# The first projection of an encoder block by blocks of 128 tokens, with the norm weight as a column scale of the weights' two parts

## What is computed

```python
h = rmsnorm(x, g_mix)                       # x / rms(x) * g_mix, per token
proj = h @ w_in                             # 512 x 1024 by 1024 x 3584
qa, ka, va, qb, kb, vb, gate_a, gate_b = split(proj)
oa = global_axial_gqa(...); ob = window_sink_gqa(...)
merged = sigmoid(gate_a) * (oa @ w_branch_a) + sigmoid(gate_b) * (ob @ w_branch_b)
x = x + merged @ w_out
x = x + moe(rmsnorm(x, g_ffn), ...)         # top 4 of 32 experts
out = rmsnorm(x, g_final)
```

## Time and profile before

| what | value |
|---|---|
| median of 3 runs | 1559.31 us (1558.9 to 1561.21) |
| the profiled execution | 1559.76 us, of which the span of the trace is 1558.0 us |
| mean granted PE clock | 0.986 |
| first matmul of the projection | 18.18 us |
| PE idle between its transposes and that matmul | 4.32 us |
| group 0 of the projection ends, group 1 begins | 42.50 us |

### The profile page before, as it was taken

How to read it: one execution, slowest core, us unless ns; L and a number is a source line. 1 busy time by engine, 2 the same in 40 slices (tenths; PEclk the granted TensorE clock), 3 DMA queues, 4 the chain that set the end, 5 groups by cost and what they waited for, 6 DMA issues and landing times.

```text
span 1558.0 us, 21230 instructions
## 1 busy us (share of the span) xinstructions
PE 1512.6 (97%) x7254; PEld 1240.9 (80%) x7287; DVE 1311.9 (84%) x1021; ACT 1091.1 (70%) x1158; POOL 268.3 (17%) x164
## 2 busy tenths in 40 slices
PE   7999999997999999999999999999999999999997
PEld 6888788886788888888888888888888888888884
DVE  4556587656899999999999999999999999999975
ACT  4344587424787777877777787787777778778772
POOL 6302144100001110111100001202120022002211
PEclk9999999998899999999999999999999999999997
DMA  8330001545999999999999999999999999999972
GB/s 299 122 100 36 1 1 55 200 141 181 378 363 391 385 389 385 379 391 379 375 387 386 386 387 381 388 390 385 376 372 391 386 378 394 387 387 380 388 263 113
DMA packets 131102, 477.36 MB, mean 306 GB/s; under 512 B 9720, under 2 KB 10240, under 8 KB 130976
## 3 DMA queue, kind: packets, MB, share of 16 engines
q1 hardware_dynamic: 117536, 434.79, 72.1%
q0 software_dynamic: 9936, 36.44, 9.1%
q10 hardware_dynamic: 3600, 5.73, 1.1%
HBM read 452.81 MB, written 24.12 MB: 306 GB/s over the span
## 4 chain that ended last, share of the span: by engine, by line
PE 93%; DVE 3%; ACT 2%; issue 1%; DMA 0%; ACTq 0%; SPq 0%; DVEq 0%
PE ps L1446 28%; PE ps L1447 28%; PE ps L1448 28%; PE ps L1708 2%; PE ps L1716 2%; PE ps L1735 2%; PE ps L1494 1%; PE ps L1537 1%; DVE pT_lo L1155 1%; PE ps L1538 0%; ACT probs L754 0%; PE ps L1479 0%; DMA xs<-in_x 0%; DVE split L1068 0%; PE ps L1515 0%
## 5 line engine op out<-in xcount | busy, mean ns | idle before, releaser
L1279 DVE TENSOR_TENSOR chunk_lo<-chunk,chunk_hi 128x2048 fp32r<-128x2048 f32 x384 | 859.3, 2285 | 39.0 <-ACT chunk_hi L879 36.0
L879 ACT ACTIVATE chunk_hi<-chunk 128x2048 fp32r<-128x2048 f32 x378 | 722.6, 1914 | 109.2 <-PE ps L1448 108.1
L1446 PE MATMUL ps<-chunk_hi,XT 128*128 128x512 f32 x1024 | 404.8, 395 | 2.0 <-DVE XT L1324 2.0
L1448 PE MATMUL ps<-chunk_hi,XT 128*128 128x512 f32 x1024 | 400.0, 391 | 0.0
L1447 PE MATMUL ps<-chunk_lo,XT 128*128 128x512 f32 x1024 | 399.9, 391 | 0.0
L644 POOL DMA_INDIRECT sum_rows<-y,idx x31 | 116.4, 3755 | 921.7 <-ACT y L985 833.8
L1446 PEld LDWEIGHTS ps<-chunk_hi,XT 128*128 128x128 f32 x1024 | 192.8, 188 | 41.1 <-DVE XT L1324 2.4
L1448 PEld LDWEIGHTS ps<-chunk_hi,XT 128*128 128x128 f32 x1024 | 192.4, 188 | 40.4
L1447 PEld LDWEIGHTS ps<-chunk_lo,XT 128*128 128x128 f32 x1024 | 192.8, 188 | 38.9
L1446 PE MATMUL ps<-chunk_hi,hidT 128*128 128x512 f32 x512 | 200.4, 391 | 0.0
L1448 PE MATMUL ps<-chunk_hi,hidT 128*128 128x512 f32 x512 | 200.1, 391 | 0.0
(11 more groups left out here) (272 smaller groups left out, 1900.7 us busy)
## 6 DMA issues: line engine op xcount, KB each, us to landing
chunk<-in_w_gate_up SPq DMA_DIRECT2D x256, 1024.0 KB, 8.8
chunk<-in_w_down SPq DMA_DIRECT2D x128, 1024.0 KB, 7.1
raw<-in_w_in SPq DMA_DIRECT2D x14, 1024.0 KB, 6.8
xs<-in_x SPq DMA_DIRECT2D x8, 512.0 KB, 5.2
w_out<-in_w_out SPq DMA_DIRECT2D x4, 1024.0 KB, 6.8
raw<-in_w_branch_a SPq DMA_DIRECT2D x2, 1024.0 KB, 6.0
raw<-in_w_branch_b SPq DMA_DIRECT2D x2, 1024.0 KB, 6.9
sum_rows<-xs ACTq DMA_DIRECT2D x4, 512.0 KB, 2.6
```

Of the source, the lines that this page charges most:

```text
L879: a.activation(chunk_hi[hi_slot(c, nxt)][:, :], chunk[c][:, :], ACT.Copy).then_inc(ex_hi, 1)
L1279: v.tensor_tensor(chunk_lo[c][:, :], chunk[c][:, :], chunk_hi[hi_slot(c, nxt, first)][:, :].bitcast(F32), ALU.subtract).then_inc(ex_lo, 1)
L1446: mm(dst, lhsT(0), rhs(0), start=start, stop=False)
L1448: return mm(dst, lhsT(1), rhs(0), start=False, stop=stop)
```

## The change

The chunks of the weights are now scaled: `gcol` goes into both parts of the weights (per k block of 512 columns, so each split is four instructions of 128x512 instead of one of 128x2048) and out of the transposed tokens. The tokens are normalised, transposed (two PSUM banks each, 4 and 5 or 6 and 7) and split one block at a time; PE starts block 0 of the projection with token block 0 alone and transposes the next token block in the middle of each of the blocks n = 0, 1, 2. Chunks 0 and 1 are split in halves with a count of `in_lo` for each half (`split_parts` turns a number of chunks into that count). SP loads x block 0, chunk 0, x block 1, chunk 1, x blocks 2 and 3, chunks 2 and 3. The five small DMAs of ACT's queue stand behind the split of chunk 2. Core of the diff:

```diff
@@ SP
-            for c in range(NT):
-                sp.dma_start(xs[:, c, :], x_v[c]).then_inc(x_in[c], 16)
+            load_x(0)
+            load_chunk(0)
+            load_x(1)
+            load_chunk(1)
+            load_x(2)
+            load_x(3)
+            load_chunk(2)
+            load_chunk(3)
+            for n in range(NIN, CHUNKS - 2):
+                sp.wait_ge(in_lo, split_parts(n - NIN + 1))
                 load_chunk(n)
@@ ACT
+            def top_part(n, kk):
+                cols = slice(kk * 512, kk * 512 + 512)
+                k = n % 2 * 4 + kk
+                return a.activation(split[:, n % NIN_SPLIT, 0, cols], raw[:, n % NIN, cols], ACT.Copy,
+                                    scale=gcol[:, k:k + 1])
...
-                a.activation(split[:, n % NIN_SPLIT, 0, :], raw[:, n % NIN, :], ACT.Copy).then_inc(in_hi, 1)
+                for kk in range(4):
+                    last = top_part(n, kk)
+                last.then_inc(in_hi, 1)
+            def hT_round(c):
+                act.wait_ge(hT_ps, c + 1)
+                a.activation(hT[:, 0, :, c * 128:(c + 1) * 128],
+                             ps[:, 4 + c % 2 * 2:6 + c % 2 * 2, :].rearrange("p t (k n) -> p (t k) n", n=128),
+                             ACT.Copy).then_inc(hT_hi, 1)
+            mix_root(0)
+            first_in_hi(0, 0)
+            first_in_hi(0, 1)
+            hT_round(0)
+            mix_root(1)
+            first_in_hi(1, 0)
+            first_in_hi(1, 1)
+            hT_round(1)
+            mix_root(2)
+            hT_round(2)
+            mix_root(3)
+            hT_round(3)
+            in_split_hi(2)
+            act.dma_start(rp, rope.rearrange("(c p) t n -> p c t n", p=128)).then_inc(consts_in, 16)
...
@@ DVE
+            def rest_part(n, kk):
+                cols = slice(kk * 512, kk * 512 + 512)
+                k = n % 2 * 4 + kk
+                return v.scalar_tensor_tensor(out=split[:, n % NIN_SPLIT, 1, cols], in0=raw[:, n % NIN, cols],
+                                              scalar=gcol[:, k:k + 1],
+                                              in1=split[:, n % NIN_SPLIT, 0, cols].bitcast(F32), op0=ALU.mult,
+                                              op1=ALU.subtract)
+            def in_split_lo(n):
+                if n >= IN_CHUNKS:
+                    return
+                dve.wait_ge(in_hi, split_parts(n + 1))
+                for kk in range(4):
+                    last = rest_part(n, kk)
+                last.then_inc(in_lo, 1)
+            mix_norm(0)
+            first_in_lo(0, 0)
+            hT_rest(0)
+            first_in_lo(0, 1)
+            mix_norm(1)
+            first_in_lo(1, 0)
+            first_in_lo(1, 1)
+            hT_rest(1)
+            mix_norm(2)
+            hT_rest(2)
+            mix_norm(3)
+            hT_rest(3)
+            in_split_lo(2)
@@ PE
                     for k in range(KD):
-                        if n == 0:
-                            pe.wait_ge(hT_lo, k + 1)
-                        elif n < 4 and k == 0:
-                            pe.wait_ge(hT_lo, KD)
+                        if n < 3 and k == 4:
+                            mix_turn(n + 1)
+                        if n < 4 and k == 0:
+                            pe.wait_ge(hT_lo, n + 1)
                         m = 2 * grp + k // 4
-                        if c == 0 and k % 4 == 0:
-                            pe.wait_ge(in_lo, m + 1)
+                        if n == 0 and k % 2 == 0:
+                            pe.wait_ge(in_lo, k // 2 + 1)
+                        elif c == 0 and k % 4 == 0:
+                            pe.wait_ge(in_lo, split_parts(m + 1))
```

More of the change, by code:

```diff
@@ L323, in encoder_block, with split_parts @@
         chunk_src += [kp(w[0, :, h * 512:(h + 1) * 512]) for h in range(2) for w in (w_branch_a, w_branch_b)]
+        def split_parts(n):
+            return n + min(n, 2)
         def blocks(t, width):
@@ L670, in _, with mix_root @@
             a.activation(warm[:, :], eps[:, :], ACT.Sqrt)
-            for c in range(NT):
+            def mix_root(c):
                 act.wait_ge(x_in[c], 16)
@@ L693, in in_split_hi @@
                     act.wait_ge(proj_ps, 4 * (m // 2) + 4)
-                a.activation(split[:, n % NIN_SPLIT, 0, :], raw[:, n % NIN, :], ACT.Copy).then_inc(in_hi, 1)
[L696 to L703, removed]
+                for kk in range(4):
+                    last = top_part(n, kk)
+                last.then_inc(in_hi, 1)
+            def hT_round(c):
[17 more added lines that the diff above has]
+            act.dma_start(rp, rope.rearrange("(c p) t n -> p c t n", p=128)).then_inc(consts_in, 16)
+            act.dma_start(gains[:, 0, :], qa_norm[0:1, :].to_broadcast([128, HD])).then_inc(consts_in, 16)
+            act.dma_start(gains[:, 1, :], ka_norm[0:1, :].to_broadcast([128, HD])).then_inc(consts_in, 16)
+            act.dma_start(sink[:, :], sink_b[0:1, :].to_broadcast([128, 8])).then_inc(consts_in, 16)
+            act.dma_start(brt[:, :], b_router[0:1, :].to_broadcast([128, E])).then_inc(consts_in, 16)
             def project_out(n):
@@ L1051, in link, with first_in_lo, mix_norm @@
                 dve.wait_ge(dve_step, steps[0])
-            for c in range(NT):
+            def rest_part(n, kk):
[12 more added lines that the diff above has]
+                last.then_inc(in_lo, 1)
+            def first_in_lo(n, half):
+                dve.wait_ge(in_hi, 2 * n + half + 1)
+                for kk in (2 * half, 2 * half + 1):
+                    last = rest_part(n, kk)
+                last.then_inc(in_lo, 1)
+            def mix_norm(c):
                 dve.wait_ge(rt_done, c + 1)
@@ L1057, in _, with hT_rest @@
                 v.tensor_scalar(xn[:, c, :], xs[:, c, :], rstd[:, c:c + 1], None, ALU.mult).then_inc(xn_ready, 1)
[L1058 to L1078, removed]
+            def hT_rest(c):
+                dve.wait_ge(hT_hi, c + 1)
+                cols = slice(c * 128, c * 128 + 128)
+                v.tensor_tensor(hT[:, 1, :, cols],
+                                ps[:, 4 + c % 2 * 2:6 + c % 2 * 2, :].rearrange("p t (k n) -> p (t k) n", n=128),
+                                hT[:, 0, :, cols].bitcast(F32), ALU.subtract).then_inc(hT_lo, 1)
+            dve.wait_ge(gcol_ps, 1)
+            v.tensor_copy(gcol[:, :], ps[:, 7, 0:KD]).then_inc(gcol_ready, 1)
+            mix_norm(0)
[11 more added lines that the diff above has]
+            in_split_lo(2)
             for n in range(NIN_SPLIT, 7):
```

30 lines of the change are left out of this document (15 added, 15 removed).

## The result

The changed kernel takes 1569.62 us (median of 4 runs, 1569.5 to 1569.74); the kernel before, in the same comparison, 1560.07 (4 runs, 1558.9 to 1561.21). The ratio is 1.0048 with a 95% interval of 1.0033 to 1.0064: slower by 0.3 to 0.6%.

The account below looks back on a forecast made before the run. PE's work plus the places where PE stands still bound the kernel; +8.5 at group 1's k = 4, +0.6 cold clock and +0.6 odd chunks gave +9.7 us, 1569.0 on the median, range 1562.5 to 1573.

Parts of the forecast that it names:

- the term of chunk 3: Group 1: DVE's parts of chunks 2 and 3 fall into POOL's chain, so k = 4 starts at 54.15, not 45.60: +8.5 us.
- the clock behind it: Behind k = 4 of group 1: PE, cold from waiting, still runs at half clock; 0 to 1.3 us lost, 0.6 taken.
- the odd chunks: Groups 2 to 6: longer ACT and DVE splits use 0.92 of 0.94 us spare; 0.6 us in all, bounds 0 and 1.3.
- The win of 2 to 3.5 us at the end of group 0: Start: PE begins with token block 0 alone, first matmul near 12.6; group 0 ends at 39 to 40.5, 2 to 3.5 us won.
- The alternation: Chunks 2 and 3: DVE and POOL exclude each other, each gap between DVE's parts admitting one POOL instruction; main case, 0.76, at 1569.
- the case held likelier: Chunk 2's first DVE part comes in the cast behind POOL's first subtraction, so its fourth part ends at 49.4, not 45.2.
- POOL's chain may start up to 1 us earlier, taken as 0: POOL's bias chain, start 25.73: ACT's small DMAs are out of its way; -1 to 0 us, taken as 0.
- the rival of the earlier chain: POOL's chain starts several us earlier, from 20 us, as its loads land sooner; chunk 3 ends near 48.5, total 1564; chance 0.06.
- four or five DVE parts of 0.66: POOL's bias chain: DVE parts of 0.66 us between its instructions delay it; the eighth part, end of chunk 3, comes at 54.1.
- some 0.7 longer: Sign in the profile: POOL's subtractions last some 0.7 us longer than 4.10 beside DVE's parts.
- The doubled form: Rival: DVE's new two-SBUF-operand form needs 2 ns an element, each part 0.5 us longer; total 1583; chance 0.02.
- The rest of the trace the old one, 9 to 10 us later: Sign in the profile: apart from the named places, the trace stays as before, shifted 9 to 10 us later.

Follow-up runs that it names:

- e4: Changed kernel with one wait added on POOL, holding the rest of its bias chain until chunks 2 to 4 are split; 1560.51 us, ratio 0.9993 to before.
- e1: Changed kernel without POOL's eight bias instructions, a memset in their place; 1560.38 us, ratio 0.9996 to before.
- e6: Kernel before, with POOL's eight bias instructions replaced by a memset; 1560.18 us, ratio 0.9999 to before.
- e2: Changed kernel with splits of chunks 2 to 13 as one unscaled 128x2048 instruction each on ACT and DVE; 1560.49 us, ratio 0.999 to before.
- e3: Kernel before, its order kept, with each chunk's split in four unscaled 128x512 instructions on ACT and DVE; 1571.4 us, ratio 1.0066 to before.
- e5: Kernel of e4 with odd chunks from 3 on handed to PE in halves, at k = 4 and k = 6; 1556.08 us, ratio 0.9968 to before.
- e8: e5 and e7 together: odd chunks in halves plus added identity transposes; 1562.57 us, ratio 0.9989 to before.
- e7: Kernel of e4 with 48 identity transposes added on PE between out-projection and first expert products; 1562.77 us, ratio 1.0006 to before.

## Why the prediction was right, step by step

The forecast was 1569.0 and slower; measured were 1569.62 and slower. The sum of the profiled execution was +9.7 against a measured +9.93. Its terms did less well than that: the term of chunk 3 was 2.5 too high, the clock behind it 0.6 too high, the odd chunks were 1.1 too low and 2.2 were missing. The mechanism is as forecast; that the total comes within 0.3 us is luck.

- **The win of 2 to 3.5 us at the end of group 0**: 3.72. The first matmul came at 12.00 (12.6 forecast); the matmuls are 0.43 us apart until 16.4, the pace of the earlier trace rows at 0.50, and 0.23 from 16.7 on (the record of the granted clock says 1.00 for this stretch, so the cold start is read from the spacing alone). It was swallowed by the wait behind it, as forecast: in e4, without that wait, it passes through.
- **The alternation**: right in kind, and shown. e1, e4 and e6 take POOL out of the way, e2 and e3 separate pieces from order; all came out on this side. Chunk 2's first part came inside the cast, the case held likelier; its fourth ended at 46.94, where 49.4 stood.
- **"POOL's chain may start up to 1 us earlier, taken as 0"**: mis-sized. It started 1.83 us earlier (23.90 against 25.73). POOL issued these loads 0.70 us earlier (11.21 for the first, 11.91 before); the rest is a faster landing. That this comes from ACT's five small DMA issues, which now follow at 30.8, fits but wasn't tried. It is the rival of the earlier chain, at 0.06, in small; it shortened the loss and didn't replace its cause.
- **"Between its instructions stand four or five DVE parts of 0.66", POOL's subtractions "some 0.7 longer"**: each part held POOL up by 0.28 to 0.35 only. POOL's next instruction is recorded from 0.07 us behind its last one, while DVE's part ends 0.55 behind it, so 0.48 is the most that such a part can cost by the records; the forecast had charged the part's whole 0.66.
- These two put the end of chunk 3 near 51.2 instead of 54.1, and k = 4 of group 1 at 51.58 (54.15 forecast): the term **+8.5** was +6.0. PE did not even wait a second time: chunk 3's last part ended at 51.22, and k = 0 to 3, mostly at half clock, took until 51.58. The term "clock behind it, 0.6" was 0.
- **Odd chunks, "0.6 in all, bounds 0 and 1.3"**: 1.70, outside the bounds. ACT's and DVE's row of chunk 5 and PE at its k = 4, from the changed kernel:

```profile
68.17 2.56 ACT L694 ACTIVATE split<-raw,gcol 128x512 fp32r<-128x512 f32 x4 [2.06 <-PE ps L1512]
...
70.76 2.74 DVE L1096 SCALAR_TENSOR_TENSOR split<-raw,gcol,split 128x512 fp32r<-128x512 f32 x4 [16.89 <-ACT split L694]
...
73.12 0.39 PE L1512 MATMUL ps<-split,hT 128*128 128x512 f32 x1
73.55 0.50 PE L1510 MATMUL ps<-split,hT 128*128 128x512 f32 x1
```

  DVE's four took 2.74, +0.45 where +0.43 was priced. ACT's four took 2.56: the 2.41 of the earlier trace rows is the same form out of PSUM, and from SBUF it is 0.15 longer, so +0.64 and not +0.49. The sum, 1.09, is over the 0.94 of slack: PE starts k = 4 0.43 behind the matmul ahead, where 0.23 is its pace, and 0.11 slower after a wait. That is 0.3 each; 0.34 was measured at each of five. A term that rests on 0.94 - 0.92 has no accuracy, and its upper bound had to be wider. e4, in which POOL's chain is out of the way, loses the same 0.34 at each. e5 settles the cause: with a half handed over at k = 4 the loss is 0.
- **A term that was missing**: +2.2 us between the out-projection and the experts, of which the last section tells.
- **The doubled form**, a rival at 2%: four parts took 2.74 us with both operands from SBUF, against 2.72 with one from PSUM; twice of that would be 5.4. The rule of the Trainium skill ("Vector Engine (DVE) Microarchitecture Reference", Points that are easy to get wrong) on scalar-tensor-tensor with two SBUF sources doesn't hold for this float32 form in the trace. The rule on the port, in contrast, agrees: by the Trainium skill ("SBUF — State Buffer", Who interferes with whom) a DVE instruction with two SBUF inputs contends with a GpSimd instruction that reads SBUF, and the ports that they share are an exclusive lock. The 4.59 us for a part of 0.74 shows it held for POOL's whole instruction. Two exceptions stand in the last section.
- **"The rest of the trace the old one, 9 to 10 us later"**: at the end yes, but 7.5 of it from the projection's end on, and only then 9.7.

## What to carry to other kernels

Where DVE instructions with both operands in SBUF work beside a chain of GpSimd casts and subtractions, as here, it is their number that counts: one 128x2048 paid one turn, four 128x512 paid four, and PE paid with a stand of 8 us. Before a step is cut into pieces or moved, look which GpSimd work runs in its new place; if that work has no reader soon, one semaphore wait ahead of it gives the whole loss back (e4). And when a hand-over with under 1 us of slack grows, hand over a part of it (e5) rather than argue about tenths.

## What the runs showed of the hardware that wasn't expected

**A stretch of half clock far from the change.** From the out-projection's last matmul to the first expert's twelfth product it is 31.09 us before and 33.33 after. In that stretch PE transposes the last token block (8 transposes) and computes its router products (16). The two rows of the kernel before, and of the changed one:

```profile
374.12 1.07 PE L1650 MATMUL ps<-ident,xn_b 128*128 128x128 f32 x8
376.21 1.94 PE L1660 MATMUL ps<-w_router,h2T 128*128 128x32 f32 x16 [1.02 <-ACT h2T L872]
```

```profile
381.63 1.87 PE L1719 MATMUL ps<-ident,xn_b 128*128 128x128 f32 x8
384.33 3.59 PE L1729 MATMUL ps<-w_router,h2T 128*128 128x32 f32 x16 [0.83 <-ACT h2T L911]
```

In the kernel before the clock falls at 378.37, 0.2 us behind the last router product; in the changed one it falls at 381.74, right after these transposes began, though the work ahead is the same. All kernels with that code line up (the last two add work only behind the 16 router products, so their last column isn't comparable and is left out):

| kernel | clock falls, us behind the out-projection | the 8 and the 16, us | stretch against before, us |
|---|---|---|---|
| before | 9.6 | 1.07 + 1.94 | 0 |
| e6 | 10.1 | 1.07 + 1.94 | +0.2 |
| e5 | 10.2 | 1.07 + 1.94 | +0.3 |
| e4 | 7.6 | 1.07 + 3.46 | +1.2 |
| e1 | 7.4 | 1.07 + 3.60 | +1.2 |
| e2 | 6.0 | 1.37 + 3.59 | +1.0 |
| changed | 5.5 | 1.87 + 3.59 | +2.2 |
| e3 | 5.4 | 1.91 + 3.59 | +2.4 |
| e8 | 7.6 | 1.07 + 3.45 | |
| e7 | 4.6 | 1.95 + 3.59 | |

So the +2.2 us is these two steps at half clock (0.80 + 1.65 = 2.45, less 0.19 of waiting between them): the out-projection's end to the first of them is 5.34 us in both kernels, and the last of them to the twelfth product 21.73 and 21.70. The position of the fall differs by 5.6 us between kernels; what sets it no run here tells. It is not the code ahead alone: up to these products e7's program is that of e4, and e8's that of e5, and yet the clock fell 4.6 and 7.6 us behind where it fell 7.6 and 10.2 behind. So the +2.2 us isn't shown to be an effect of the change, though the four executions of the changed kernel agree within 0.24 us. A comparison of two kernels can hold up to 2.4 us of this beside the effect of the change, and e5's gain holds 0.9 us of it against e4's. In the kernels without added transposes, but for e2, the clock comes back 0.6 to 1.1 us ahead of the twelfth product. That speaks against e7's expectation, which took the length of half clock for the cause and the fall for one at "about 5 us" in every run: the length seems to follow from where the fall lies.

**A GpSimd instruction beside which two operands from SBUF don't wait.** DVE's split of chunk 2 in the kernel before, two SBUF operands, takes its full-speed 2.29 us beside POOL's TENSOR_SCALAR of 96x1024, and a piece of e3 takes its 0.69 beside it (27.45 to 28.14, POOL's from 25.43 to 28.23); the casts and subtractions behind it exclude each time. It doesn't leave every DVE instruction alone: in e7 the norm's scale of token block 3, alone 0.75 us, ends 0.56 behind it:

```profile
24.22 2.80 POOL L554 TENSOR_SCALAR bias<-bias 96x1024 f32<-96x1024 f32 x1 [11.49 <-DMA bias<-in_b_gate_up]
...
26.61 0.96 DVE L1121 TENSOR_SCALAR xn<-xs,rstd 128x1024 f32<-128x1024 f32 x1
```

Why isn't settled.

**An instruction with one SBUF operand that waits too.** In the changed kernel the norm's scale of token block 3 takes 2.21 us beside POOL's cast (26.77 to 28.66), where the same form takes 0.75 elsewhere (0.75 at 20.64):

```profile
27.00 2.21 DVE L1119 TENSOR_SCALAR xn<-xs,rstd 128x1024 f32<-128x1024 f32 x1
```

It waits even for a POOL instruction that reads nothing. In the kernel before:

```profile
8.26 1.80 POOL L521 MEMSET bias_new<- 32x2048 bf16 x1
...
9.68 0.93 DVE L1057 TENSOR_SCALAR xn<-xs,rstd 128x1024 f32<-128x1024 f32 x1
```

This ends 0.55 behind POOL, as the parts do behind a cast. Beside the same MEMSET of the changed kernel (7.76 to 9.56) two parts of chunk 0, with two operands from SBUF, take 0.75 and 0.74: they don't wait. So two operands aren't a condition for the exclusion, and which POOL instruction excludes depends on the form of DVE's. This float32 form runs at 0.73 ns an element, where those with two operands take 1.1 to 1.3. The trace shows the waits, not the reason.

ACT shows no such wait: its four parts of chunk 3, beside POOL's subtraction, take the 2.56 us that they take elsewhere.
